# Which of the eight FFN down blocks is computed plainly: the first in place of the last, with the shared sums added slab by slab inside the last block

## The chip, the cores and the metric

One core of one Trainium2 chip runs the whole kernel. The metric is the device time of the kernel in microseconds (us). TensorE does the matrix products, VectorE and ScalarE the elementwise work, GpSimd part of the weight splitting, and SyncE's and ScalarE's queues issue the transfers.

## The reference, cut to what matters

Two transformer-like blocks run one after the other on 1024 tokens of width 1024. The change lies in the feed-forward part of the second one and in the gate behind it:

```
m = rmsnorm(h, g_mlp[i])
h = h + jnp.square(jax.nn.relu(m @ w_up[i])) @ w_down[i]     # D_FF = 4096
gate = jax.nn.sigmoid(rmsnorm(h, g_ple[i]) @ w_ple_gate[i])
h = h + gate * (p[i] @ w_ple_proj[i])
return rmsnorm(h, g_final)
```

## The kernel before, in words

**Numbers.** All products are made with split operands: a float32 value x is a high part (rounded to the format that TensorE multiplies) and a low part x minus high. A product is then three matmuls: high weight by high data, high weight by low data, low weight by high data. For weights ScalarE or GpSimd makes the high part, GpSimd the low part (`down_hi`, `down_part`, `plain_slab`), in a ring of eight entries (`w_hi`, `w_lo`) that TensorE frees as it goes. Weights come in slabs of 512 KB through SyncE's queue (`next_slab`) into a stage of two places; the transfer of a slab waits until the slab two before it is split.

**Up.** `f = relu(...)^2` is made in 16 pairs of feature tiles. Pairs 0 and 1 are plain, pairs 2 to 15 use a scheme with seven products in place of eight (`up_pair`; its products are numbered 1, 6, 5, 7, 2, 3, 4, the order `SEVEN`). Product 3 goes into the bank of product 5 and waits until VectorE has read that one (`c22`, L3367). Each finished pair is stored to DRAM (`f_kept`).

**Down.** The 4096 features are eight blocks of two pairs. In four slabs (s = 0 to 3) a block adds to `H`, each slab to two of its eight tiles. Blocks 0 to 6 use the seven-product scheme (`down`): 4 slabs of 7 products of 6 matmuls. For that VectorE and ScalarE must make, from the two stored pairs ("u"): four sums and differences (`diff`), seven high parts (`u_hi`), seven low parts (`u_lo`). And VectorE makes four sums of weights for each slab (`weight_sums`, behind the first addition of the slab before). VectorE adds each product into `H` or into `SHARED`, a sum that three of the four quarters of an output have in common (`down_added`). The work for block b+1 is spread over slabs 1 to 3 of block b (`next_u_steps`). A product can wait for VectorE: 2, 3 and 4 go into the banks of 1, 5 and 7 of the same slab:

```python
BANK = {1: 0, 2: 0, 6: 1, 5: 2, 3: 2, 7: 3, 4: 3}
BEFORE = {2: 1, 3: 5, 4: 7}
                    if j in BEFORE:
                        pe.wait_ge(s_dr, product_turn(b, s, BEFORE[j]))
```

Block 7 is plain (`last_down`): 4 slabs of 48 matmuls, with only four high and four low parts of u (1, 8, 2, 3) and no sums. While TensorE does it, VectorE adds `SHARED` into `H` (`shared_added`, 12 additions), adds the plain products, and finishes tile after tile of `H` for the gate (`last_tile`: `raw_lo`, L3276, and `raw_add`, L3285, with ScalarE's `raw_hi` and `raw_square` ahead of them). The projection (`PJ`, 4 MB) is loaded by ScalarE's queue at the end of block 6.

**Behind it.** The gate product (`product`, L991, on `XH2` and `XL2`) takes tile k of the data in order; `square_total` follows its first slab. The additions are counted by `s_dr`, the freed ring entries by `s_we`.

Every engine goes through its own instruction list in order, so an operation that waits holds all behind it on that engine.

Of the kernel before, what the change touches and what calls it, by code (L numbers as in the profile page):

```python
# [197 lines left out]
FFN_ORDER += [("down", _b, _s) for _b in range(DOWN_BLOCKS) for _s in range(4)]  # L198
FFN_ORDER += [("last", FFN_BLOCKS - 1, _s) for _s in range(4)]
# [27 lines left out]
for _n in range(pair_slab(PAIRS), N_PLE - 4):  # L227
    _uses(_n, 7, {6: _n + 1}, 1)
LAST_FREED = _freed
USED += USED[-1:] * (-len(USED) % RING)  # L230
for _n in range(N_PLE - 4, NSLAB):
    ENTRY[_n] = len(USED)
    USED += [("slab", _n + 1)] * 4
assert all(ENTRY[_n] % 4 == 0 for _n in range(N_PLE - 4, NSLAB))
DOWN_ADDS = 28 * DOWN_BLOCKS
# [61 lines left out]
def product_turn(b, s, j):  # L297
    return 7 * (4 * b + s) + SEVEN.index(j) + 1
# [23 lines left out]
def program(nc, x_t, pos, w, vec, rows, consts, p_t, out):  # L322
    ctx = ExitStack()
    with ctx:
# [146 lines left out]
        def head_square_at(k):  # L471
# [25 lines left out]
        u_even_at = {1: raw_at, 4: raw_at + 8 * kb, 5: xh_at + 48 * kb, 3: xh_at + 56 * kb, 6: xh_at, 2: xh_at + 8 * kb, 7: xh_at + 16 * kb}  # L497
        u_odd_at = {1: raw_at + 16 * kb, 6: raw_at + 24 * kb, 5: raw_at + 32 * kb, 7: raw_at + 40 * kb,
                    2: xh_at + 32 * kb, 3: xh_at + 40 * kb, 4: xh_at + 24 * kb}
        u_plain_at = {8: xh_at + 24 * kb, 1: xh_at + 32 * kb, 2: xh_at + 40 * kb, 3: xh_at + 48 * kb}  # L500
        u_at = {"even": u_even_at, "odd": u_odd_at, "plain": u_plain_at, "later": {5: raw_at + 48 * kb}}
        U_SPLIT = {(name, j): place(at_, f"ffn_u_{name}{j}", [P, 2, 2, HB], F32R)[0] for name, table in u_at.items() for j, at_ in table.items()}
        U_WHOLE = {(name, j): place(at_, f"ffn_whole_u_{name}{j}", [P, 2, 2, HB], F32)[0] for name, table in u_at.items() for j, at_ in table.items()}
        PJ = (place(xh_at, "ple_proj_a", [P, 6, TOK], F32)[0], place(xh_at + 56 * kb, "ple_proj_b", [P, 2, TOK], F32)[0])
# [21 lines left out]
        def u_name(b, j):  # L526
            if b == DOWN_BLOCKS:
                return "plain", j
            if b % 2:
                return "odd", j  # L530
            return "later" if j == 5 and b else "even", j
# [105 lines left out]
        s_hk = sem("h_kept_then_ffn_plain_u_loaded")  # L637
# [41 lines left out]
        s_u7 = Part(s_hk, 16 * KT)  # L679
# [59 lines left out]
        def _(sp):  # L739
# [57 lines left out]
            next_slab(d0)  # L797
            next_slab(d0 + 1)
# [6 lines left out]
            used(pair_use(p, 1))  # L805
            load(0, 3)
            used(pair_use(p, 2))
            load(0, 2)
            store(p, 0)
            store(p, 1)  # L810
            for b in range(DOWN_BLOCKS):
                if b == 0:
                    used(pair_use(p, 6))
                    stored(4)
                else:
                    sp.wait_ge(s_slab, FFN_AT["down", b - 1, 3] + 1)
                    stored(2 * b + 4)
# [4 lines left out]
            for n in range(d0 + 4 * DOWN_BLOCKS + 2, NSLAB):  # L822
                next_slab(n)
# [11 lines left out]
        def _(pool):  # L835
# [100 lines left out]
            def down_part(d, i):  # L936
                n, j = d0 + d, SEVEN[i]
# [10 lines left out]
            d0 = pair_slab(PAIRS)  # L948
            for c in range(2 * PLAIN_PAIRS):
                plain_slab(N_FFN + c, c)  # L950
            for p in range(PLAIN_PAIRS, PAIRS):
                for i in range(7):
                    pair_part(p, i)
            for d in range(4 * DOWN_BLOCKS):
                for i in range(7):
                    down_part(d, i)
            for turn, n in enumerate(range(N_PLE - 4, NSLAB)):
                plain_slab(n, 2 * PLAIN_PAIRS + turn)
# [11 lines left out]
        class Down:  # L970


            def wait(self, eng, k):
                eng.wait_ge(s_dr, DOWN_ADDS + k + 1)

        @block.tensor
        def _(pe):
# [724 lines left out]
            def down(b, s):  # L1702
                n = FFN_AT["down", b, s]
                e, d = ENTRY[n], 4 * b + s
                for i, j in enumerate(SEVEN):
# [19 lines left out]
            def last_down(q):  # L1725
                n = FFN_AT["last", FFN_BLOCKS - 1, q]
                e0 = ENTRY[n]
                pe.wait_ge(s_w_ready, 4 * (n + 1))
                if q == 0:
                    s_ul.wait(pe, len(LOWS))  # L1730
                    pe.wait_ge(s_dr, DOWN_ADDS - 7)
                elif q == 1:
                    pe.wait_ge(s_dr, DOWN_ADDS)
                for e in range(2):
                    if q >= 2:
                        pe.wait_ge(s_dr, DOWN_ADDS + 2 * (q - 2) + e + 1)
# [2031 lines left out]
```

## Time and profile before

| | |
|---|---|
| median of 3 runs | 2628.53 us (2624.53 to 2628.74) |
| profiled execution: time, span | 2624.4 us, 2622.5 us |
| granted TensorE clock, mean | 0.995 |
| busy: TensorE, VectorE, ScalarE, GpSimd | 97%, 66%, 44%, 43% |
| seven-product blocks of down begin at 2191.70 us, the plain one at 2472.09 us, the gate product at 2515.61 us | |

A duration is that of one instruction as the profile has it; instructions of one engine that follow each other without a gap overlap in the records by some 0.08 us on VectorE, so what counts on an engine that is never idle is the distance from start to start. "[2.31 <-DVE ffn_t L3367]" behind a row means that the engine sat idle for 2.31 us before it, until VectorE's instruction of line 3367 that writes ffn_t was done.

### The profile page before, as it was taken

The page shows a single profiled execution, that of the slowest core. Times are in us where ns is not written, and L with a number is a line of the kernel's source. Part 1 is how long each engine was busy: PE and PEld are TensorE (multiplying, and loading weights), DVE is VectorE, ACT ScalarE, POOL GpSimd, SP SyncE. Part 2 cuts the span into 40 slices and gives each one's busy share as a digit, 9 for nine tenths or more (in the row PEclk, how much of TensorE's full clock was granted, in tenths as well). Part 3 has the DMA queues.
Part 4 walks back from the last instruction along what each step waited for, and adds up shares of the span by engine and source line. Part 5 has one row for each costly group of instructions (what it writes and reads, how often), then busy time and mean ns, then how long its engine had stood idle before and what let it go on. Part 6 is the DMA issues. An engine that isn't in the chain of part 4 may idle for free.

```text
span 2622.5 us, 33254 instructions
## 1 busy us (share of the span) xinstructions
PE 2542.3 (97%) x12712; PEld 2022.7 (77%) x12712; DVE 1730.9 (66%) x2061; ACT 1147.0 (44%) x1757; POOL 1136.2 (43%) x1100
## 2 busy tenths in 40 slices
PE   8999999999999999999999999999999998999997
PEld 7877888687787787887676777767888887878886
DVE  7636763677748648658776455565556668999856
ACT  3527882336405305316275545463333334444232
POOL 4633344532342432432441222214645556777652
PEclk9999999999999999999999999999999999999999
DMA  3111002212212112111230001002133333322412
GB/s 140 49 44 33 25 25 86 92 47 101 65 49 81 57 48 73 64 49 61 84 129 25 33 25 33 25 25 97 49 126 107 113 113 121 121 98 104 161 41 81
DMA packets 58137, 189.93 MB, mean 72 GB/s; under 512 B 5952, under 2 KB 6336, under 8 KB 57984
## 3 DMA queue, kind: packets, MB, share of 16 engines
q1 hardware_dynamic: 44704, 143.67, 16.1%
q10 hardware_dynamic: 13280, 44.17, 4.7%
q8 instruction: 102, 1.67, 0.3%
q14 instruction: 51, 0.42, 0.1%
HBM read 158.33 MB, written 29.49 MB: 72 GB/s over the span
## 4 chain that ended last, share of the span: by engine, by line
PE 80%; DVE 11%; ACT 5%; issue 3%; POOL 1%; ACTq 0%; DMA 0%; DVEq 0%; POOLq 0%; SPq 0%
PE PS L991 38%; PE PS L1697 10%; PE PS L1720 8%; PE PS L1321 4%; PE PS L1228 3%; PE PS L1742 2%; PE PS L1554 1%; PE PS L1537 1%; PE PS L1354 1%; PE PS L1127 1%; PE PS L1364 1%; PE PS L1358 1%; PE PS L1141 1%; PE PS L1577 1%; PE PS L1670 1%
## 5 line engine op out<-in xcount | busy, mean ns | idle before, releaser
L839 POOL CAST w_hi<-w_stage 128x1024 fp32r<-128x1024 f32 x130 | 144.4, 1111 | 1046.9 <-PE PS L991 756.9
L842 POOL TENSOR_TENSOR w_lo<-w_stage,w_hi 128x256 fp32r<-128x256 f32 x520 | 494.0, 981 | 10.4
L991 PE MATMUL PS<-XH,w_hi 128*128 128x512 f32 x1216 | 386.6, 399 | 9.0 <-ACT ssd_z L2136 3.3
L991 PE MATMUL PS<-XL,w_hi 128*128 128x512 f32 x1216 | 375.5, 390 | 0.0
L991 PE MATMUL PS<-XH,w_lo 128*128 128x512 f32 x1216 | 375.0, 390 | 0.0
L991 PEld LDWEIGHTS PS<-XH,w_hi 128*128 128x128 f32 x1216 | 221.4, 188 | 65.5 <-issue 12.9
L991 PEld LDWEIGHTS PS<-XL,w_hi 128*128 128x128 f32 x1216 | 228.2, 188 | 48.8
L991 PEld LDWEIGHTS PS<-XH,w_lo 128*128 128x128 f32 x1216 | 228.2, 188 | 48.6
L946 POOL TENSOR_TENSOR w_lo<-w_sums,w_hi 128x256 fp32r<-128x256 f32 x112 | 126.1, 1138 | 59.7 <-ACT w_hi L2482 59.1
L1697 PE MATMUL PS<-ffn_token_sums,w_hi 128*128 128x512 f32 x448 | 138.0, 389 | 0.0
L1720 PE MATMUL PS<-ffn_u_even,w_hi 128*128 128x512 f32 x400 | 125.6, 395 | 5.3 <-DVE ffn_shared L3477 3.2
L934 POOL TENSOR_TENSOR w_lo<-up_w_sums,w_hi 128x512 fp32r<-128x512 f32 x56 | 82.7, 1478 | 80.7 <-ACT w_hi L2470 80.5
L2096 ACT ACTIVATE ssd_x<-ssd_conv 128x1024 f32<-128x1024 f32 x16 | 16.9, 1060 | 227.2 <-DVE ssd_conv L2924 222.5
L1697 PE MATMUL PS<-ffn_raw,w_hi 128*128 128x512 f32 x336 | 104.7, 393 | 2.3 <-DVE ffn_t L3367 2.3
L1720 PE MATMUL PS<-ffn_u_odd,w_hi 128*128 128x512 f32 x336 | 104.3, 392 | 1.1 <-DVE H L3479 0.4
L3479 DVE TENSOR_TENSOR H<-H,PS 128x512 f32<-128x512 f32 x140 | 93.4, 679 | 17.0 <-PE PS L1720 15.5
L1697 PEld LDWEIGHTS PS<-ffn_token_sums,w_hi 128*128 128x128 f32 x448 | 84.1, 188 | 17.4
L1720 PEld LDWEIGHTS PS<-ffn_u_even,w_hi 128*128 128x128 f32 x400 | 74.8, 190 | 25.4 <-issue 7.7
L2924 DVE SCALAR_TENSOR_TENSOR ssd_conv<-PS,VC,ssd_conv 128x1023 f32<-128x1023 f32 (+2 forms) x72 | 92.3, 1282 | 2.6
L2922 DVE TENSOR_SCALAR ssd_conv<-PS,VC 128x1024 f32<-128x1024 f32 x24 | 32.2, 1343 | 92.6 <-PE PS L991 92.5
L3240 DVE TENSOR_TENSOR sb_z<-sb_z,PS 128x1024 f32<-128x1024 f32 (+3 forms) x48 | 45.8, 954 | 67.3 <-PE PS L1554 67.0
L946 POOL TENSOR_TENSOR w_lo<-w_stage,w_hi 128x256 fp32r<-128x256 f32 x84 | 82.5, 990 | 15.3 <-ACT w_hi L2482 15.3
(492 smaller groups left out, 6105.1 us busy)
## 6 DMA issues: line engine op xcount, KB each, us to landing
w_stage<-w SPq DMA_DIRECT2D x202, 512.0 KB, 3.3
ssd_sum_rows<-sums_kept ACTq DMA_DIRECT2D x32, 512.0 KB, 3.8
f_kept<-ffn_t SPq DMA_DIRECT2D x32, 512.0 KB, 2.6
ffn_whole_u_even<-f_kept SPq DMA_DIRECT2D x16, 512.0 KB, 4.8
ffn_whole_u_odd<-f_kept SPq DMA_DIRECT2D x12, 512.0 KB, 5.4
H<-x_t ACTq DMA_DIRECT2D x8, 512.0 KB, 8.2
pj_kept<-ple_proj_tiles ACTq DMA_DIRECT2D x8, 512.0 KB, 2.6
h_kept<-H ACTq DMA_DIRECT2D x8, 512.0 KB, 3.6
```

Source lines behind the costliest of these rows:

```text
L839: nc.gpsimd.tensor_copy(w_hi[:, slot, :, :], w_stage[:, slot, :, :]).then_inc(s_w_hi, 1)
L842: nc.gpsimd.tensor_tensor(w_lo[:, slot, k:k + 2, :], w_stage[:, slot, k:k + 2, :], w_hi[:, slot, k:k + 2, :].bitcast(F32), ALU.subtract).t ...
L934: nc.gpsimd.tensor_tensor(ring(w_lo, e, 2), src, ring(w_hi, e, 2).bitcast(F32), ALU.subtract).then_inc(done, count)
L946: nc.gpsimd.tensor_tensor(ring(w_lo, e), src, ring(w_hi, e).bitcast(F32), ALU.subtract).then_inc(done, count)
L991: mm = nc.tensor.matmul(outs[:, half, :], wt[:, slot, k, :], a[:, k - first, half * HB:(half + 1) * HB], start=(k == whole[0] and wt is w_ ...
L1228: mm = nc.tensor.matmul(PS[:, 2 * (n % 2) + half, :], wt[:, n % 2, k, :], a[:, k, half_cols(half)], start=(k == 0 and wt is w_hi and a is ...
L1321: mm = nc.tensor.matmul(PS[:, half, :], wt[:, n % 2, k, :], a[:, k, half * HB:(half + 1) * HB], start=(k == 0 and wt is w_hi and a is XH), ...
L1697: mm = nc.tensor.matmul(PS[:, 4 * (p % 2) + BANK[j], :], ring(wt, e + 2 * i + k // 2, k % 2), up_acts(j, hl, k), start=(j not in BEFORE an ...
L1720: mm = nc.tensor.matmul(PS[:, 4 * (d % 2) + BANK[j], :], ring(wt, e + i, k), down_acts(b, j, k, hl), start=(j not in BEFORE and k == 0 and ...
L1742: mm = nc.tensor.matmul(PS[:, 4 * (q % 2) + 2 * e + half, :], ring(wt, e0 + k // 2, k % 2), down_acts(DOWN_BLOCKS, quad, t % 2, hl), start ...
L2924: ins = v.scalar_tensor_tensor(out=y[:, d:TOK], in0=src[:, 0:TOK - d], scalar=wcol(3 - d), in1=y[:, d:TOK], op0=ALU.mult, op1=ALU.add)
L3479: v.tensor_tensor(dst, dst, src, ALU.add).then_inc(s_dr, 1)
```

## The change

The order of the eight blocks is turned over at its ends. Block 0 is the plain one and comes first; blocks 1 to 7 use the seven-product scheme.

- At the end of the last up pair VectorE and ScalarE make only the four high and four low parts of block 0; the `diff`, `u_hi` and `u_lo` of block 1 are made while TensorE does the plain block, between the plain additions.
- Block 7 prepares no u. In its slabs VectorE does the three additions of `SHARED` for that slab behind product 6, the tile 2s-1 behind product 5, and the tile 2s behind product 4 (ScalarE's `gate_acts` are put between its `down_hi`).
- `PJ` is loaded by SyncE's queue: two tiles (1 MB) behind the loads of u at the start of block 1, six (3 MB) near the end of block 7. The places of u in memory are dealt out anew.

```diff
-FFN_ORDER += [("down", _b, _s) for _b in range(DOWN_BLOCKS) for _s in range(4)]
-FFN_ORDER += [("last", FFN_BLOCKS - 1, _s) for _s in range(4)]
+FFN_ORDER += [("plain", 0, _s) for _s in range(4)]
+FFN_ORDER += [("down", _b, _s) for _b in range(1, FFN_BLOCKS) for _s in range(4)]
...
                 for j in (1, 8, 3, 2):
                     load(b + 1, j)
-                for s in range(2, 6):
-                    next_slab(d0 + 4 * b + s)
+                if b == 1:
+                    sp.dma_start(PJ[0][:, :, :], pj_kept[0:2, :, :].rearrange("k p t -> p k t")).then_inc(s_pl, 16)
+                for c in range(2, 6):
+                    next_slab(n + c)
+            for n in range(PLAIN_DOWN + 4 * DOWN_BLOCKS + 2, N_PLE + 2):
+                next_slab(n)
+            used(USED[ENTRY[N_PLE - 1] + 2])
+            sp.dma_start(PJ[1][:, :, :], pj_kept[2:8, :, :].rearrange("k p t -> p k t")).then_inc(s_pl, 16)
...
-            def last_down(q):
+            def plain_down(q):
...
                     for t in range(4):
                         k = 4 * e + t
+                        if k % 2 == 0:
+                            pe.wait_ge(s_w_ready, 4 * n + k // 2 + 1)
+                        if q == 0 and e == 0 and t % 2 == 0:
+                            s_ul.wait(pe, t + 2)
...
+                    if not highs and d % 4 and i == 5:
+                        gate_acts(2 * (d % 4 - 1))
+                    if not highs and d % 4 > 1 and i == 1:
+                        gate_acts(2 * (d % 4 - 1) - 1)
...
+            def shared_added(s):
+                dve.wait_ge(s_dr, product_turn(FFN_BLOCKS - 1, s, 6))
+                for h in (H[:, 2 * s + 1, HB:TOK], H[:, 2 * s, HB:TOK], H[:, 2 * s + 1, 0:HB]):
+                    v.tensor_tensor(h, h, SHARED[:, s, :], ALU.add).then_inc(s_dv.sem, 1)
...
+                    if end and i == 1:
+                        shared_added(s)
+                    if end and s and i == 2:
+                        last_tile(2 * s - 1)
+                    if end and i == 6:
...
+                        last_tile(2 * s)
...
                 if last:
-                    diff(5, 0)
                     u_lo(1, 0)
-                    diff(6, 0)
+                    u_lo(8, 0)
...
+            diff(5, 1)
+            diff(6, 1)
+            plain_even(0)
+            diff(7, 1)
+            diff(4, 1)
+            u_lo(1, 1)
+            plain_odd(0)
```

## Rows read from the trace of the kernel before

**Rows 1.** The page, part 4: the chain that ended last, by engine

```profile
PE 80%; DVE 11%; ACT 5%; issue 3%; POOL 1%; ACTq 0%; DMA 0%; DVEq 0%; POOLq 0%; SPq 0%
```

**Rows 2.** Timeline of TensorE: start, duration, instruction, count, [idle before <- releaser]

```profile
2181.84 0.39 PE L1697 MATMUL PS<-ffn_raw,w_lo 128*128 128x512 f32 x1
2184.53 0.70 PE L1697 MATMUL PS<-ffn_raw,w_hi 128*128 128x512 f32 x2 [2.31 <-DVE ffn_t L3367]
...
2191.70 0.62 PE L1720 MATMUL PS<-ffn_u_even,w_hi 128*128 128x512 f32 x2
...
2202.35 1.19 PE L1720 MATMUL PS<-ffn_u_even,w_hi 128*128 128x512 f32 x2 [3.25 <-DVE ffn_shared L3477]
...
2237.79 0.61 PE L1720 MATMUL PS<-ffn_u_odd,w_hi 128*128 128x512 f32 x2
...
2434.01 0.62 PE L1720 MATMUL PS<-ffn_u_even,w_hi 128*128 128x512 f32 x2
...
2472.09 1.07 PE L1742 MATMUL PS<-ffn_u_plain,w_hi 128*128 128x512 f32 x4
...
2515.61 0.62 PE L991 MATMUL PS<-raw_hi,w_hi 128*128 128x512 f32 x2
```

**Rows 3.** Two stretches: length, busy time of each engine (instructions), granted clock, DMA share, GB/s

```profile
2192.00:2240.00 48.00, 43.20 (x178) 33.63 (x177) 45.51 (x63) 21.62 (x42) 34.57 (x32) 0.96 0.33 114
2240.00:2280.00 40.00, 39.44 (x172) 31.78 (x172) 37.17 (x57) 17.25 (x35) 30.00 (x29) 1.00 0.32 110
```

**Rows 4.** Timeline of VectorE in the last up pair

```profile
2177.30 1.23 DVE L3416 TENSOR_TENSOR ffn_whole_u_even<-ffn_whole_u_even,ffn_whole_u_even 128x1024 f32<-128x1024 f32 x1 [2.43 <-DMA ffn_whole_u_even<-f_kept]
2178.56 2.21 DVE L3422 TENSOR_TENSOR ffn_u_even<-ffn_whole_u_even,ffn_u_even 128x1024 fp32r<-128x1024 f32 x1
2180.69 2.31 DVE L3416 TENSOR_TENSOR ffn_whole_u_even<-ffn_whole_u_even,ffn_whole_u_even 128x1024 f32<-128x1024 f32 x1
...
2183.70 0.69 DVE L3367 TENSOR_TENSOR ffn_t<-ffn_t,PS 128x512 f32<-128x512 f32 x1
```

**Rows 5.** Timeline of VectorE in the down blocks and behind them

```profile
2436.43 0.68 DVE L3479 TENSOR_TENSOR ffn_shared<-ffn_shared,PS 128x512 f32<-128x512 f32 x1
2437.03 0.41 DVE L3448 TENSOR_TENSOR w_sums<-w_stage 128x256 f32<-128x256 f32 x1
...
2438.49 0.68 DVE L3479 TENSOR_TENSOR ffn_shared<-ffn_shared,PS 128x512 f32<-128x512 f32 x1
...
2445.70 0.66 DVE L3448 TENSOR_TENSOR w_sums<-w_stage 128x256 f32<-128x256 f32 x1
...
2472.30 0.69 DVE L3479 TENSOR_TENSOR H<-H,PS 128x512 f32<-128x512 f32 x1 [0.67 <-PE PS L1720]
2473.02 8.40 DVE L3489 TENSOR_TENSOR H<-H,ffn_shared 128x512 f32<-128x512 f32 x12
```

**Rows 6.** Three lines of VectorE: duration in ns, min/median/max

```profile
L3489 DVE TENSOR_TENSOR H<-H,ffn_shared x12: 676/678/1231, 2473.0 to 2480.7; 128x512 f32<-128x512 f32 x12
...
L3276 DVE SCALAR_TENSOR_TENSOR raw_lo<-H,VC,raw_hi x8: 1277/1478/1758, 2484.3 to 2519.7; 128x1024 fp32r<-128x1024 f32 x8
...
L3285 DVE TENSOR_TENSOR square_sum<-square_sum,ffn_t x12: 1218/1410/1761, 1832.7 to 2521.4; 128x1024 f32<-128x1024 f32 x12
```

**Rows 7.** SyncE's queue at block 6: issues, the two slabs' landing times; PJ

```profile
2434.21 2.51 SPq L782 DMA_DIRECT2D ffn_whole_u_plain<-f_kept  x4
2436.76 7.31 SPq L758 DMA_DIRECT2D w_stage<-w  x2
...
DMA to landing us min/median/max: 3.2/5.6/7.9
...
ple_proj_a<-pj_kept ACTq DMA_DIRECT2D x1, 3072.0 KB, 11.5
```

**Rows 8.** Timeline of TensorE: two gaps elsewhere, and the pace behind each

```profile
1769.99 0.73 PE L1554 MATMUL PS<-sb_softplus_hi,from_r 128*128 128x512 f32 x2 [1.65 <-DVE sb_softplus_lo L3258]
...
1778.67 0.94 PE L1554 MATMUL PS<-sb_softplus_hi,from_r 128*128 128x512 f32 x2 [2.24 <-DVE sb_softplus_lo L3258]
```

More of the change, by code:

```diff
@@ L526, in u_name, with u_loaded @@
         def u_name(b, j):
-            if b == DOWN_BLOCKS:
+            if b == 0:
                 return "plain", j
-            if b % 2:
-                return "odd", j
-            return "later" if j == 5 and b else "even", j
+            if b == 1 and j == 4:
+                return "first", j
+            return ("even", "odd")[b % 2], j
+        def u_loaded(b):
+            return 16 * (b // 2 + 1)
         def down_acts(b, j, i, hl):
@@ L805, in _ @@
             used(pair_use(p, 1))
+            load(0, 2)
             load(0, 3)
-            used(pair_use(p, 2))
-            load(0, 2)
             store(p, 0)
@@ L815, in _ @@
                 else:
[L816 to L817 removed]
+                    sp.wait_ge(s_slab, n)
+                    stored(PAIRS)
                 for j in (1, 8, 3, 2):
                     load(b + 1, j)
[L820 to L822 removed]
+                if b == 1:
[6 more added lines that the diff above has]
+            sp.dma_start(PJ[1][:, :, :], pj_kept[2:8, :, :].rearrange("k p t -> p k t")).then_inc(s_pl, 16)
+            for n in range(N_PLE + 2, NSLAB):
                 next_slab(n)
@@ L953, in _ @@
                     pair_part(p, i)
+            for c in range(4):
+                plain_slab(PLAIN_DOWN + c, 2 * PLAIN_PAIRS + c)
             for d in range(4 * DOWN_BLOCKS):
@@ L956, in _ @@
                     down_part(d, i)
-            for turn, n in enumerate(range(N_PLE - 4, NSLAB)):
-                plain_slab(n, 2 * PLAIN_PAIRS + turn)
+            for c, n in enumerate(range(N_PLE, NSLAB)):
+                plain_slab(n, 2 * PLAIN_PAIRS + 4 + c)
         class Tiles:
@@ L1750, in _ @@
                 up_pair(p)
-            for b in range(DOWN_BLOCKS):
+            for q in range(4):
+                plain_down(q)
+            for b in range(1, FFN_BLOCKS):
                 for s in range(4):
                     down(b, s)
-            for q in range(4):
-                last_down(q)
             for k in range(KT - 2):
@@ L2554, in _ @@
                 raw_square(ple, k)
+            for d in range(4 * DOWN_BLOCKS):
+                b = d // 4 + 1
+                highs = [j for j, b_ in HIGHS if b_ == b + 1]
+                for i in range(7):
+                    down_hi(d, i)
+                    if highs and d % 4 == 2 and i in (1, 3, 5):
+                        u_hi(highs[i // 2], b + 1)
+                    if highs and d % 4 == 3 and i in (1, 2, 4, 6):
+                        u_hi(highs[(1, 2, 4, 6).index(i) + 3], b + 1)
+                    if not highs and d % 4 and i == 5:
+                        gate_acts(2 * (d % 4 - 1))
+                    if not highs and d % 4 > 1 and i == 1:
+                        gate_acts(2 * (d % 4 - 1) - 1)
+            for k in range(5, KT):
+                gate_acts(k)
             raw_root(ple)
@@ L3475, in down_added @@
                         dve.wait_ge(s_dr, product_turn(b, s, 1 if j == 6 else 5))
-                    if j == 1 and b == 0:
+                    if end and j in (5, 3, 4):
+                        s_dv.wait(dve, 3 * s + {5: 1, 3: 2, 4: 3}[j])
+                    if j == 1 and b == 1:
                         v.tensor_copy(dst, src).then_inc(s_dr, 1)
```

210 lines of the change are left out of this document (81 added, 129 removed).

## Prediction

> **What bounds the kernel now.** I read the chain that ended last first: 80% of it is TensorE [rows 1], so the question is only where TensorE stands still, before and after. Then the timeline of TensorE at the block borders [rows 2]. From 2472.09 to 2515.61 the plain block runs 192 matmuls in 43.52 us, 0.2267 us each, without a pause; a product of six is 1.36 us, a slab of seven products 9.52, a block of four slabs 38.08. Against that pace the seven-product blocks show three things: block 0 takes 46.09 us (2191.70 to 2237.79), blocks 1 to 5 take 39.24 each (196.22 from 2237.79 to 2434.01), block 6 takes 38.08 (to 2472.09). VectorE is busy 37.17 of 40 us in blocks that prepare the next one [rows 3], so the 1.16 us that such a block loses is VectorE's; block 6 prepares only the light plain block and loses nothing. The gate product follows the plain block with no gap [rows 2].
>
> Ahead of block 0 TensorE loses more: the last matmul of product 2 of the last pair begins at 2181.84, and at full pace the 24 matmuls of products 3 and 4 would end at 2182.07 + 5.44 = 2187.51; they end at 2191.70. The wait of 2.31 us is for `c22`; VectorE came late to it because `diff`, `u_lo` and `diff` took from 2177.30 to 2183.0, the first behind a load, the other two at 2.2 and 2.3 us [rows 4]. In block 0 the longest wait, 3.25 us, is for the first addition, behind five low parts of u [rows 2], and the granted clock is 0.96 of full there [rows 3].
>
> **The change part by part.**
>
> *1. Entry into down: 11.0 us go.* Now only four high and low parts stand there. `u_lo` 1 can run from 2177 on, `u_lo` 8 about 1.2 us later; at 1.2 us each (they are 1024 wide like the 1.23 of [rows 4]) `c22` ends near 2181, before TensorE wants product 3 at 2182.07. If the second takes 2.2 us, TensorE waits up to 1 us. The last pair then saves 2191.70 - 2187.51 = 4.19. The plain block (43.52) needs nothing more of VectorE; there VectorE has 4 `diff`, 7 `u_lo` and 8 additions of 1.2 us and one `weight_sums`, 24 us, in 43.5, even if the loads of block 1's u come 8 us after the start. Block 1 then meets a VectorE that is free. In the sum: before, down was 46.09 + 5 x 39.24 + 38.08 + 43.52 = 323.9; after it is 43.52 + 6 x 39.24 + 38.08 + L = 317.0 + L, where six blocks (1 to 6) again prepare the next one and L is what block 7 loses. So 6.85 + 4.19 = 11.0 us are gained, bounds 10.0 and 11.0, less L.
>
> *2. Block 7: VectorE's work on the tiles now stands in front of TensorE: L = 10.8 us.* Before, `shared_added` and the tiles ran beside the plain block, which has no `BEFORE` waits within a slab. Now they stand between the addition of product 6 and those of 5 and 7, and TensorE's products 3 and 4 wait for exactly those two. Prices per instruction, start to start: an addition 0.60, four weight sums 1.46, an addition of `SHARED` 8.40 / 12 = 0.70 [rows 5]; `raw_lo` 1.30 and `raw_add` 1.22, the middle between shortest and median less the overlap of 0.08 [rows 6]. Block 6 shows VectorE taking up product 1 of a block 2.4 us after its start (2436.43 against 2434.01), because it still ends the block before [rows 2, 5]; so it will be at block 7. From the start of block 7 to the addition of product 7 in slab 3 VectorE has 25 additions (15.0), three `weight_sums` (4.4), twelve `SHARED` additions with four waits of 0.09 for product 6's sum (8.8), six `raw_lo` (7.8), five `raw_add` (6.1): 42.1. With 2.4 before, and 2.8 of waits for products (1.4 in slab 0, 0.7 in each of 1 and 2, mostly product 4, which cannot start before 7 is added), product 7 is added at 47.4. TensorE follows 0.14 later (`c22` ended at 2184.39, product 3 began at 2184.53 [rows 2, 4]) and needs 1.36: the block ends at 48.9 in place of 38.1. TensorE's gaps, walked slab by slab, are 1.3 us in slab 0 and pairs of 1.0 + 1.8, 2.3 + 1.8 and 0.9 + 1.8 in the others.
>
> Bounds: with the shortest durations everywhere (`SHARED` 0.60, `raw_lo` 1.20, `raw_add` 1.14) L is 8.6; with the medians of [rows 6] (1.40, 1.33) 11.9. What comes behind costs nothing: VectorE ends tile 7 at about 54, and TensorE wants it with the eighth step of the gate's first slab, at 48.9 + 9.5 = 58.4.
>
> *3. The clock.* A gap of 1.65 us was followed by two matmuls in 0.73 us, one of 2.24 by two in 0.94, and that of 3.25 by two in 1.19, against 0.62 at full pace [rows 2, 8]. The gap of 2.3 in slab 2 is at the edge. If the clock falls from 2.4 to 1.2 GHz for one product the loss hides in the wait that follows; if it falls at the 1.8 gaps too, product 4 takes twice 1.36 and the block 2.6 more. I take 0.5, bounds 0 and 2.6.
>
> *4. 1 MB of `PJ` in SyncE's queue: 2.0 us.* At block 6 the four loads of u go out from 2434.21, the first slab behind them at 2436.76, landing 7.9 us later, 10.7 after the block's start [rows 7]; VectorE wants it at 2445.70, 11.7 after [rows 5]. Only 1 us is to spare. 3 MB of `PJ` took 11.5 us [rows 7], so 1 MB takes up to 3.8; in front of the slab it brings it to 13.3 to 14.5. VectorE then stands at `weight_sums` for 2 to 3 us in slab 1 of block 1, with the additions for the product banks behind it, and in a block in which it has no slack. I take 2.0, since the transfers overlap in part; bounds 0 (the slab is not behind `PJ` after all) and 3.8. The other 3 MB go out some 9 us before the gate product and are used 11 us into it or later, and the slab behind them is wanted 21.8 us in: hidden, by about 8 us.
>
> *5. At nothing:* matmuls, transfers and splits are as many as before; `plain_down` now waits for its weights by quarters, which can only be earlier. ScalarE is at 17 of 40 us in blocks that prepare u [rows 3]; block 7 has none of those seven activations, and `gate_acts` puts up to four into a slab, ahead of high parts of weights that TensorE takes a slab later.
>
> Sum: -11.0 + 10.8 + 0.5 + 2.0 = +2.3 us on a profiled execution of 2624.4 us (span 2622.5). The median of the runs shown is 4.1 higher, so I put it on that: 2628.5 + 2.3 = 2630.8 us.
>
> **The rivals.**
>
> *Likeliest: an exchange of stalls.* The entry's stall goes, and block 7 gets one of the same size: 2631, in its own range 2626 to 2637 (all low: -11.0 + 8.6 = -2.4; all high: -10.0 + 11.9 + 2.6 + 3.8 = +8.3). Within 0.2% (5.3 us, about what a measurement of this kernel can tell from no change).
>
> *Faster.* The entry gains 11.0, and block 7 holds TensorE for less than 5 us. That needs the tile work to come later than I place it: if VectorE did it only beside the gate product, L would be the part of `SHARED` alone (1.3 in slab 0 and some 0.4 in two others, 2 in all), and the time 2628.5 - 11.0 + 2 = 2619.5, with the slab at `PJ` on time. For it: VectorE has 8 us to spare behind block 7. Against it: `last_tile` stands in front of the addition of 7 in the instruction order, and only its waits, not its place, can move. It decides at L + PJ below 5.7 us.
>
> *Slower by the clock.* In block 7 the pairs of gaps add up to 2.8, 4.1 and 2.7 us with one product between them. If that is enough for the lower level in slabs 1 to 3, and at the wait in block 1 as well, then -11.0 + 14.5 + 3.8 = +7.3: 2636. It decides when more than one slab of block 7 runs product 4 at 1.2 GHz.
>
> *Slower by contention.* `raw_lo` is 1.28 at its shortest and 1.76 at its longest, the addition of `SHARED` 0.68 and 1.23 [rows 6]; the long ones lie where GpSimd works. If all those in block 7 are long (`SHARED` 1.15, the others 1.68), L is 20.8 and the time 2628.5 - 11.0 + 20.8 + 2.0 = 2640. It would take GpSimd's work beside nearly each of them; GpSimd is busy 30 of 40 us in the down blocks [rows 3]. Against it: the medians are 1.48 and 0.68. The Trainium skill (GPSIMD Engine Reference, section 1, Specifications) says that GpSimd's SBUF interfaces are shared with VectorE and contended by instructions with two SBUF inputs. That speaks against this change, since the operations that it moves are of that kind and the additions that stay are not; the spread of the durations agrees with it.
>
> *The entry is not cured.* If `c22` is still late because the load of u lands later than 2177, 4 of the 11 us stay: 2635.
>
> **How the numbers follow.** Exchange 0.53. Faster 0.15. Clock 0.14, contention 0.10, entry not cured 0.08. Of the exchange a few per cent spill to the slow side, of the three slow ones about a quarter stays within 0.2%; faster 0.15, same 0.57, slower 0.28. The range 2622 to 2640 cuts off half of the faster case and the far end of contention.
>
> **What would show it.** The plain block begins near 2187.5 and lasts 43.5 us; no `c22` gap. Block 1 lasts some 41 us, with a wait for w_stage at VectorE's `weight_sums` in slab 1. Blocks 2 to 6 last 39.2. Block 7 lasts 47 to 50 us, with TensorE waiting for the additions of H. The gate product follows without a gap. Wrong would be: block 7 near 40 us (faster), or above 52 (slower), or a plain block that starts at 2191.

## The result, and the profile of the changed kernel

The changed kernel takes 2634.55 us (median of 7 runs, 2632.95 to 2637.3) against 2627.09 us (7 runs, 2624.53 to 2628.74) for the kernel before on the same chip: a ratio of 1.0029, 95% interval 1.0017 to 1.0041. It is slower, by 0.3%, 7.5 us. The forecast was +2.3 us, 2630.8 on a base of 2628.5, with a range of 2622 to 2640. The range holds the time, and the sign is the one forecast, but the likeliest outcome (0.57) was a change within 0.2%; slower than that had 0.28.

In the chain that ended last, TensorE has 75% and VectorE 14% [rows 1 had 80% and 11%]:

```profile
PE 75%; DVE 14%; ACT 5%; issue 4%; POOL 1%; DMA 0%; ACTq 0%; SPq 0%; DVEq 0%; POOLq 0%
```

The block borders, from the timeline of TensorE (start, duration, instruction, count, idle before it and its releaser); L1704 is the last up pair (products 2, 3 and 4 begin at 2181.99, 2184.71 and 2187.43), L1749 the plain block, L1727 the seven-product blocks, L998 the gate product:

```profile
2181.99 0.61 PE L1704 MATMUL PS<-ffn_raw,w_hi 128*128 128x512 f32 x2
...
2184.71 0.61 PE L1704 MATMUL PS<-ffn_raw,w_hi 128*128 128x512 f32 x2
...
2187.43 0.61 PE L1704 MATMUL PS<-ffn_token_sums,w_hi 128*128 128x512 f32 x2
...
2190.15 1.07 PE L1749 MATMUL PS<-ffn_u_plain,w_hi 128*128 128x512 f32 x4
...
2233.67 0.62 PE L1727 MATMUL PS<-ffn_u_odd,w_hi 128*128 128x512 f32 x2
...
2251.62 0.70 PE L1727 MATMUL PS<-ffn_u_odd,w_hi 128*128 128x512 f32 x2 [1.47 <-DVE H L3478]
...
2274.98 0.39 PE L1727 MATMUL PS<-ffn_u_even,w_hi 128*128 128x512 f32 x1
...
2471.03 0.62 PE L1727 MATMUL PS<-ffn_u_odd,w_hi 128*128 128x512 f32 x2
...
2480.51 1.05 PE L1727 MATMUL PS<-ffn_u_odd,w_hi 128*128 128x512 f32 x2 [2.52 <-DVE H L3478]
...
2496.46 0.70 PE L1727 MATMUL PS<-ffn_u_odd,w_hi 128*128 128x512 f32 x2 [1.86 <-DVE H L3478]
...
2498.04 1.05 PE L1727 MATMUL PS<-ffn_u_odd,w_hi 128*128 128x512 f32 x2
...
2510.76 0.70 PE L1727 MATMUL PS<-ffn_u_odd,w_hi 128*128 128x512 f32 x2 [1.84 <-DVE H L3478]
...
2525.33 0.70 PE L1727 MATMUL PS<-ffn_u_odd,w_hi 128*128 128x512 f32 x2 [2.07 <-DVE H L3478]
...
2526.80 0.63 PE L998 MATMUL PS<-raw_hi,w_hi 128*128 128x512 f32 x2
```

Read against [rows 2]: the last pair's product 3 starts at 2184.71 and product 4 ends 5.44 us later at 2190.15, the 24 matmuls at full pace and with no gap. Before, product 3 could have started at 2182.07, waited 2.31 us, and product 4 ended 9.63 us later, at 2191.70: 4.19 us are saved. The plain block takes 43.52. Block 1 takes 2274.98 - 2233.67 = 41.31. Blocks 2 to 6 take (2471.03 - 2274.98) / 5 = 39.21 each. Block 7 takes 2526.80 - 2471.03 = 55.77 where TensorE's work is 38.08: L is 17.7 us, forecast at 10.8. The gate product follows without a gap.

The spans of the two profiled runs differ by 10.7 us (2633.2 against 2622.5). The parts: entry -11.0, block 7 +17.7, block 1 +2.1, five blocks at 39.21 in place of 39.24 -0.2, behind the gate's start -0.5; the other 2.6 us are already there where product 3 of the last pair could start (2184.71 against 2182.07), ahead of all that was changed. Over all the profiled runs of this case the start of the plain block, where it comes first, scatters from 2188.5 to 2192.6 us, so that a single span is good to about 2 us only; borders within one trace are compared below.

Two stretches of VectorE in block 7, slab 0 and slab 3 (L3478 additions of products, L3457 additions of SHARED, L3277 `raw_lo`, L3286 `raw_add`):

```profile
2476.22 3.54 DVE L3457 TENSOR_TENSOR H<-H,ffn_shared 128x512 f32<-128x512 f32 x3
2479.69 2.06 DVE L3478 TENSOR_TENSOR H<-H,PS 128x512 f32<-128x512 f32 x3
...
2518.17 2.72 DVE L3457 TENSOR_TENSOR H<-H,ffn_shared 128x512 f32<-128x512 f32 x3
2520.81 0.68 DVE L3478 TENSOR_TENSOR H<-H,PS 128x512 f32<-128x512 f32 x1
2521.41 1.85 DVE L3277 SCALAR_TENSOR_TENSOR raw_lo<-H,VC,raw_hi 128x1024 fp32r<-128x1024 f32 x1
2523.17 1.41 DVE L3286 TENSOR_TENSOR square_sum<-square_sum,ffn_t 128x1024 f32<-128x1024 f32 x1
```

and GpSimd at slab 0:

```profile
2475.51 2.58 POOL L952 TENSOR_TENSOR w_lo<-w_sums,w_hi 128x256 fp32r<-128x256 f32 x3 [1.98 <-ACT w_hi L2488]
2478.05 1.17 POOL L952 TENSOR_TENSOR w_lo<-w_stage,w_hi 128x256 fp32r<-128x256 f32 x1
2479.18 1.17 POOL L952 TENSOR_TENSOR w_lo<-w_sums,w_hi 128x256 fp32r<-128x256 f32 x1
```

Three additions of SHARED take 3.54 us in slab 0, 1.18 each, while GpSimd makes low parts the whole time; the forecast had 2.1. The additions that read a product from PS (L3478) take no longer beside the same work: 0.67 to 0.69 each in the whole trace. In slab 1 the same three take 1.90, with GpSimd idle from 2490.4 to 2491.9. TensorE's first two matmuls behind the gap of 2.52 take 1.05 us against 0.62 at full pace.

### The profile page after: what moved, and what is told of

It is laid out like the page before. It is cut to its first block, busy times and chain, and to the rows that moved or that the text cites. A ratio compares the mean times of both kernels' runs of the same rounds, so it can differ in the third digit from the quotient of the medians.

```text
span 2633.2 us, 33267 instructions
## 1 busy us (share of the span) xinstructions
PE 2548.1 (97%) x12712; PEld 2026.9 (77%) x12712; DVE 1731.8 (66%) x2061; ACT 1147.1 (44%) x1757; POOL 1138.8 (43%) x1100
## 4 chain that ended last, share of the span: by engine, by line
PE 75%; DVE 14%; ACT 5%; issue 4%; POOL 1%; DMA 0%; ACTq 0%; SPq 0%; DVEq 0%; POOLq 0%
PE PS L998 38%; PE PS L1704 10%; PE PS L1328 4%; PE PS L1727 3%; PE PS L1235 3%; PE PS L1749 2%; DVE H L3478 2%; PE PS L1561 1%; PE PS L1134 1%; PE PS L1544 1%; PE PS L1361 1%; PE PS L1371 1%; PE PS L1365 1%; PE PS L1148 1%; PE PS L1584 1%
## 5 line engine op out<-in xcount | busy, mean ns | idle before, releaser
L998 PE MATMUL PS<-XH,w_hi 128*128 128x512 f32 x1216 | 387.6, 400 | 9.0 <-ACT ssd_z L2143 3.3
L998 PE MATMUL PS<-XL,w_hi 128*128 128x512 f32 x1216 | 376.2, 391 | 0.0
L998 PE MATMUL PS<-XH,w_lo 128*128 128x512 f32 x1216 | 375.6, 390 | 0.0
L998 PEld LDWEIGHTS PS<-XH,w_hi 128*128 128x128 f32 x1216 | 222.0, 188 | 65.5 <-issue 12.5
L998 PEld LDWEIGHTS PS<-XL,w_hi 128*128 128x128 f32 x1216 | 228.9, 188 | 48.9
L998 PEld LDWEIGHTS PS<-XH,w_lo 128*128 128x128 f32 x1216 | 228.6, 188 | 48.6
L1727 PE MATMUL PS<-ffn_u_odd,w_hi 128*128 128x512 f32 x432 | 138.0, 401 | 13.2 <-DVE H L3478 12.4
L1704 PE MATMUL PS<-ffn_token_sums,w_hi 128*128 128x512 f32 x448 | 137.9, 389 | 0.0
L1727 PEld LDWEIGHTS PS<-ffn_u_odd,w_hi 128*128 128x128 f32 x432 | 82.1, 193 | 36.3 <-POOL w_lo L952 10.3
L1727 PE MATMUL PS<-ffn_u_even,w_hi 128*128 128x512 f32 x336 | 104.3, 392 | 1.1 <-DVE H L3478 0.6
L3478 DVE TENSOR_TENSOR H<-H,PS 128x512 f32<-128x512 f32 x140 | 93.0, 678 | 18.4 <-PE PS L1727 17.1
L1704 PE MATMUL PS<-ffn_raw,w_hi 128*128 128x512 f32 x336 | 103.4, 389 | 0.0
L1704 PEld LDWEIGHTS PS<-ffn_token_sums,w_hi 128*128 128x128 f32 x448 | 84.1, 188 | 17.3
```

Source lines behind the costliest of these rows:

```text
L998: mm = nc.tensor.matmul(outs[:, half, :], wt[:, slot, k, :], a[:, k - first, half * HB:(half + 1) * HB], start=(k == whole[0] and wt is w_ ...
L1704: mm = nc.tensor.matmul(PS[:, 4 * (p % 2) + BANK[j], :], ring(wt, e + 2 * i + k // 2, k % 2), up_acts(j, hl, k), start=(j not in BEFORE an ...
L1727: mm = nc.tensor.matmul(PS[:, 4 * (d % 2) + BANK[j], :], ring(wt, e + i, k), down_acts(b, j, k, hl), start=(j not in BEFORE and k == 0 and ...
L3478: v.tensor_tensor(dst, dst, src, ALU.add).then_inc(s_dr, 1)
```

## The experiments

All times are compared with runs of the kernel before on the same chip: 2625.94 us (25 runs) for the first four kernels, 2626.36 us (28 runs) for the other four.

**Experiment 1: PJ behind the slabs.**

```diff
-                if b == 1:
-                    sp.dma_start(PJ[0][:, :, :], pj_kept[0:2, :, :].rearrange("k p t -> p k t")).then_inc(s_pl, 16)
                 for c in range(2, 6):
                     next_slab(n + c)
+                if b == 1:
+                    sp.dma_start(PJ[0][:, :, :], pj_kept[0:2, :, :].rearrange("k p t -> p k t")).then_inc(s_pl, 16)
```

> Only the 1 MB of PJ moves, behind the four slabs that SyncE's queue issues in block 1. If the 1.47 us gap of TensorE in slab 1 of block 1 comes from that transfer standing ahead of the slab, block 1 goes from 41.31 to 39.2 us and the time falls by 2.1 us (about 2632.5 against 2634.6). Rival: the gap comes from VectorE's own work in the first seven-product block (it enters with the plain block's last additions); then block 1 stays at 41.3 and the time at 2634.6. Block 7 stays at 55.8 in both.

Block 1 falls from 41.31 to 39.17 us (2232.00 to 2271.17), as blocks 2 to 6. Its gap in slab 1 is gone. The changed kernel and this one, VectorE in slab 1 of block 1:

```profile
2246.33 0.43 DVE L3440 TENSOR_TENSOR w_sums<-w_stage 128x256 f32<-128x256 f32 x1 [0.89 <-DMA w_stage<-w]
...
2247.13 0.96 DVE L3443 TENSOR_TENSOR w_sums<-w_stage 128x256 f32<-128x256 f32 x1
2248.01 0.96 DVE L3445 TENSOR_TENSOR w_sums<-w_stage,w_sums 128x256 f32<-128x256 f32 x1
```

```profile
2243.69 0.42 DVE L3440 TENSOR_TENSOR w_sums<-w_stage 128x256 f32<-128x256 f32 x1
...
2244.49 0.42 DVE L3443 TENSOR_TENSOR w_sums<-w_stage 128x256 f32<-128x256 f32 x1
2244.82 0.42 DVE L3445 TENSOR_TENSOR w_sums<-w_stage,w_sums 128x256 f32<-128x256 f32 x1
```

The wait for the slab is 0.89 us, and two of the sums that it pushed back take 0.96 in place of 0.42, another 1.1: GpSimd makes low parts beside them, from 2246.95 to 2248.69. The device time is 2633.51 us, ratio 1.0032 (1.0020 to 1.0043). The ratio does not show the 2.1 us; its interval is 6 us wide. The length of block 1 shows it, and all traces agree: 40.5 to 41.8 us where PJ stands ahead of the slabs (six traces), 39.14 to 39.17 where it does not (three). Block 7 takes 56.10 us here against 55.77, which is how much the same block differs between two traces.

**Experiment 2: the product additions first.** In block 7 the SHARED additions and the tile 2s-1 go behind the addition of product 7; their waits are changed to fit.

```diff
-                    if end and i == 1:
+                    if end and i == 3:
                         shared_added(s)
-                    if end and s and i == 2:
-                        last_tile(2 * s - 1)
+                        if s:
+                            last_tile(2 * s - 1)
...
```

> In block 7 the additions of product 5 and 7 come first on VectorE; the three SHARED additions and the tile 2s-1 come behind product 7. VectorE's work is the same, only its order differs. If L is set by the place of this work (it stands between product 6's addition and those that TensorE's products 3 and 4 wait for), the waits of VectorE for late products (0.8 to 2.7 us a slab) go and slab 3's share of SHARED and tile 5 falls behind product 7: by my walk with the durations of the trace after, block 7 falls from 55.8 to some 50 us, L from 17.7 to about 10 to 12 and the time by 6 to 7.5 us. Rival: L is only the sum of VectorE's work (clock and contention decide), then only the last slab's part, 2.7 + 3.6 us at most, is gained behind the block, and comes back as a wait of the gate product.

Block 7 falls from 55.77 to 51.71 us, L to 13.6; 2630.5 us, ratio 1.0018 (1.0009 to 1.0027). That is 4.1 of the expected 6 to 7.5 us. The rival allowed a gain in the last slab only, to come back as a wait of the gate product. Neither is so: slab 3 begins 37.3 us after the block in place of 41.9, it is itself no shorter (14.4 in place of 13.9), and the gate product runs without a gap. Place matters, but the stall has only moved: TensorE now waits at product 2 for the addition of product 1, which stands behind the tile of the slab before.

```profile
2486.33 0.70 PE L1727 MATMUL PS<-ffn_u_odd,w_hi 128*128 128x512 f32 x2 [1.09 <-DVE H L3478]
...
2498.94 0.77 PE L1727 MATMUL PS<-ffn_u_odd,w_hi 128*128 128x512 f32 x1 [4.20 <-DVE ffn_shared L3478]
...
2514.80 1.19 PE L1727 MATMUL PS<-ffn_u_odd,w_hi 128*128 128x512 f32 x2 [3.18 <-DVE ffn_shared L3478]
```

VectorE is busy 48.7 of the 51.7 us: in this order the block is nearly as long as VectorE's work. Of the 3.1 us in which it is idle, 1.8 are three waits for `raw_hi`, which ScalarE, idle until then, can begin only when VectorE has added product 3; the walk had left that out.

**Experiment 3: filling TensorE's gaps.** In block 7, ahead of the waits of products 3 and 4:

```diff
+                    if b == FFN_BLOCKS - 1 and i >= 5:
+                        for _ in range({5: 4, 6: 8}[i]):
+                            nc.tensor.matmul(PS[:, 4 * ((d + 1) % 2), :], ring(w_hi, e + i, 0), down_acts(b, j, 0, 0), start=True, stop=True)
```

> In block 7 TensorE makes 4 matmuls ahead of product 3's wait and 8 ahead of product 4's, into banks of the other parity that nothing reads, so that it stands still for under 1 us at a time. Additional work: 48 matmuls that belong to no result. Clock theory: the stretches at 0.43 us a matmul behind the gaps of 2.52, 1.86 and 1.84 us go, block 7 falls by some 2.9 us to 52.9, the granted clock there is 1.0. Rival (the slow products only fill a time in which VectorE would have been the bound anyway): block 7 falls by less than 1 us, although the clock is full; and if the fillers outlast a gap it grows by up to 0.5 us a slab.

The granted clock of block 7 rises from 0.91 to 1.00, no product runs at 0.43 us a matmul, and block 7 falls by 1.6 us, to 54.19 (2471.62 to 2525.81). The window of the changed kernel's block 7 and of this one's (length, busy time and instructions of TensorE, weight loads, VectorE, ScalarE, GpSimd, granted clock, DMA share, GB/s):

```profile
2471.03:2526.80 55.77, 44.80 (x170) 34.41 (x169) 49.88 (x68) 19.76 (x34) 35.32 (x36) 0.91 0.25 89
```

```profile
2471.62:2525.81 54.19, 50.56 (x218) 40.08 (x216) 49.31 (x68) 19.95 (x34) 35.14 (x36) 1.00 0.26 89
```

VectorE's busy time is 0.6 us shorter here, since other operations fell beside GpSimd's, so the clock's part is some 1.0 to 1.6 us: less than the 2.9 of one theory, and at or above the other's bound of 1. Two traces of the same block differ by 0.3 us (experiment 1). The device time does not resolve it (2634.5 us, ratio 1.0029, interval 1.0018 to 1.0040).

**Experiment 4: GpSimd made short.** In block 7, and for the weights of the gate, GpSimd handles 8 columns of 128:

```diff
...
+                c = 8 if d >= 4 * (DOWN_BLOCKS - 1) else 128
-                nc.gpsimd.tensor_tensor(ring(w_lo, e), src, ring(w_hi, e).bitcast(F32), ALU.subtract).then_inc(done, count)
+                nc.gpsimd.tensor_tensor(ring(w_lo, e)[:, :, 0:c], src[:, :, 0:c], ring(w_hi, e).bitcast(F32)[:, :, 0:c], ALU.subtract).then_inc(done, count)
```

> GpSimd's low parts for block 7's weights, and its high and low parts for the gate's slabs, are made of 8 columns in 128 (that part of the work is left out, the output is not the reference's); all instructions, waits and transfers stay. Contention theory: in block 7 the SHARED additions fall to 0.68 us each, raw_lo to 1.28 and raw_add to 1.2; by my account of the trace after, 4.3 us of block 7's 55.8 go, and a part of the 2.9 us of slow clock with them since the gaps get shorter: block 7 at 49 to 51.5. Rival: the durations stay long since ScalarE or the transfers cause them: block 7 stays at 55.8.

Block 7 falls from 55.77 to 46.63 us (2473.40 to 2520.03), by 9.1: more than either side of the expectation. 2624.56 us, ratio 0.9997 (0.9988 to 1.0006). L is 8.55. Groups of VectorE's instructions in block 7 of the changed kernel (count, busy us, mean ns, idle before):

```profile
L3478 DVE TENSOR_TENSOR H<-H,PS 128x512 f32<-128x512 f32 x22 | 14.3, 678 | 4.9 <-PE PS L1727 4.8
L3457 DVE TENSOR_TENSOR H<-H,ffn_shared 128x512 f32<-128x512 f32 x12 | 10.1, 891 | 0.1
L3277 DVE SCALAR_TENSOR_TENSOR raw_lo<-H,VC,raw_hi 128x1024 fp32r<-128x1024 f32 x6 | 8.2, 1374 | 0.0
L3286 DVE TENSOR_TENSOR square_sum<-square_sum,ffn_t 128x1024 f32<-128x1024 f32 x4 | 6.2, 1540 | 0.0
```

Block 7 of this kernel, the window and the groups:

```profile
2473.40:2520.03 46.63, 39.94 (x169) 31.00 (x168) 43.46 (x67) 19.96 (x34) 13.07 (x34) 1.00 0.25 79
```

```profile
L3481 DVE TENSOR_TENSOR H<-H,PS 128x512 f32<-128x512 f32 x21 | 13.7, 678 | 2.4 <-PE PS L1730 2.3
L3280 DVE SCALAR_TENSOR_TENSOR raw_lo<-H,VC,raw_hi 128x1024 fp32r<-128x1024 f32 x6 | 7.7, 1278 | 0.0
L3460 DVE TENSOR_TENSOR H<-H,ffn_shared 128x512 f32<-128x512 f32 x12 | 7.7, 691 | 0.1
...
L3289 DVE TENSOR_TENSOR square_sum<-square_sum,ffn_t 128x1024 f32<-128x1024 f32 x4 | 4.9, 1228 | 0.0
```

The additions from PS take 678 ns in both; the others fall to about their shortest values. VectorE is busy 43.46 us in place of 49.88, 6.4 less: 5.7 by shorter durations, 0.7 by one addition of block 6 fewer in the window. It waits 2.5 us less for products; together 8.9 of the 9.1. The granted clock is 1.00, and the longest gap 1.58 us: what experiment 3 gave back is within these 9.1, not beside them. The rival, that ScalarE or the transfers stretch VectorE, is excluded: ScalarE is busy 19.96 us against 19.76, and the DMA share is 0.25 in both.

**Experiment 5: a plain block at both ends.** From the changed kernel; block 7 becomes plain again with SHARED, tiles and PJ as in the kernel before, blocks 1 to 6 keep the seven-product scheme.

```diff
-PAIRS, PLAIN_PAIRS, DOWN_BLOCKS = 2 * FFN_BLOCKS, 2, FFN_BLOCKS - 1
+PAIRS, PLAIN_PAIRS, DOWN_BLOCKS, END = 2 * FFN_BLOCKS, 2, FFN_BLOCKS - 2, FFN_BLOCKS - 1
...
             for q in range(4):
-                plain_down(q)
-            for b in range(1, FFN_BLOCKS):
+                plain_down(0, q)
+            for b in range(1, END):
                 for s in range(4):
                     down(b, s)
+            for q in range(4):
+                plain_down(END, q)
```

> The plain block comes first, as in the changed kernel, and block 7 is plain as well, as in the kernel before: blocks 1 to 6 use the seven-product scheme, SHARED and the tiles are done beside the plain block 7, PJ is loaded by ScalarE's queue as before. One seven-product block less: 24 matmuls more in all. So the entry's gain stands alone, and its price is the second plain block. By the sum of the prediction without L: the last pair 4.19 us shorter, down 43.52 + 5 x 39.21 + 38.08 + 43.52 = 321.2 against 323.9: 6.9 us faster than the kernel before, about 2619. Rival (the entry's gain is an illusion of the trace and lies elsewhere, or the plain block at the end meets new waits): within 2 us of the kernel before.

2619.44 us (10 runs, 2617.14 to 2622.58), ratio 0.9978 (0.9968 to 0.9987): 6.9 us faster than the kernel before by the medians, 3.4 to 8.4 by the interval, which holds the 6.9 worked out, and faster than both kernels of this study. The borders:

```profile
2188.53 0.84 PE L1752 MATMUL PS<-ffn_u_plain,w_hi 128*128 128x512 f32 x3
...
2232.05 0.62 PE L1728 MATMUL PS<-ffn_u_odd,w_hi 128*128 128x512 f32 x2
...
2427.74 0.61 PE L1728 MATMUL PS<-ffn_u_even,w_hi 128*128 128x512 f32 x2
...
2465.82 0.84 PE L1752 MATMUL PS<-ffn_u_end,w_hi 128*128 128x512 f32 x3
...
2509.34 0.61 PE L999 MATMUL PS<-raw_hi,w_hi 128*128 128x512 f32 x2
```

43.52, five blocks of 39.14, 38.08, 43.52: 320.8 us where the kernel before has 323.9, with 5.4 us (24 matmuls of 0.2267) more of TensorE's work in it. With the last pair's 4.19 us that makes 7.3 in the trace.

**Experiment 6: the tiles behind block 7.** The SHARED additions stay. ScalarE's part of the tiles (`gate_acts`) moves behind the block as well.

```diff
-                    if end and s and i == 2:
-                        last_tile(2 * s - 1)
...
-                        last_tile(2 * s)
...
-            last_tile(KT - 1)
+            for k in range(KT):
+                last_tile(k)
```

> As the changed kernel, but all eight tiles (raw_hi, raw_square, raw_lo, raw_add) come behind block 7; the SHARED additions stay in it. It prices the two parts of L apart. Prediction's working: L of SHARED alone is 2 us with its shortest durations; with 1.15 us each where GpSimd works, about 4: block 7 at 40 to 42.5 us in place of 55.8, so the tiles are 13 us or more of the 17.7. The gate product then waits for its tiles: eight of them at about 2.6 us each against the 9.5 us of its first slab, 12 to 16 us more there, and the time is within 4 us of the changed kernel's. Rival (place of SHARED is the cause, the tiles lie in time that TensorE would lose anyway): block 7 stays above 50 us.

2634.15 us, ratio 1.0030 (1.0018 to 1.0042): the same time as the changed kernel. But block 7's products end at 2518.44, 47.0 us after 2471.44: L of SHARED alone is 8.9 us, not 2 and not 4; the rival's block above 50 us did not come either. The gate product then starts 2.5 us late, and its first slab takes 17.1 us (2520.97 to 2538.06) in place of 10.9 (2526.80 to 2537.70), where 12 to 16 us had been expected. It loses 8.7 us together, and 8.9 + 8.7 = 17.6 is what block 7 lost in the changed kernel. The twelve additions of SHARED in this kernel, by line; shortest, median and longest in ns:

```profile
L3453 DVE TENSOR_TENSOR H<-H,ffn_shared x12: 877/1220/1274, 2476.6 to 2513.6; 128x512 f32<-128x512 f32 x12
```

Nearly all of them now fall beside GpSimd's work, so 8.9 is the price of SHARED with stretched durations. The tiles cost about the same in both places: with this order, moving them only chose which wait shows them.

**Experiment 7: copies on GpSimd in place of subtractions.**

```diff
...
+                if d >= 4 * (DOWN_BLOCKS - 1):
+                    nc.gpsimd.tensor_copy(ring(w_lo, e), src).then_inc(done, count)
+                else:
...
```

> As the changed kernel, but for block 7's weights and the gate's first two slabs GpSimd makes its second part with a copy of the weights (one input) in place of the subtraction (two inputs), at full width; this part of the work is left out and the output is not the reference's. If what stretches VectorE's operations is GpSimd's reading of two inputs, they fall to 0.69 (SHARED) and 1.28 (raw_lo) as with the short operations, and block 7 to about 47 us. If any work of GpSimd at full width does it, they stay near 0.9 and 1.37 on average and block 7 falls only as far as the copies are shorter than the subtractions: 52 us or more.

Block 7 is 48.48 us (2472.29 to 2520.77), near the two-input side; 2626.36 us, ratio 1.0001 (0.9992 to 1.0010). At the place in slab 0 where three additions of SHARED took 3.54 us beside subtractions, they take 2.10 beside copies; VectorE's row and then GpSimd's rows of this kernel:

```profile
2477.03 2.10 DVE L3463 TENSOR_TENSOR H<-H,ffn_shared 128x512 f32<-128x512 f32 x3
```

```profile
2476.30 1.68 POOL L956 CAST w_lo<-w_sums 128x256 fp32r<-128x256 f32 x3 [2.30 <-ACT w_hi L2494]
2478.48 0.90 POOL L956 CAST w_lo<-w_stage 128x256 fp32r<-128x256 f32 x1 [0.50 <-ACT w_hi L2494]
```

But the mean of `raw_lo` stays at 1.35 us (SHARED 0.74), GpSimd, with copies, is busy 22.6 us in place of 35.3, and two of TensorE's waits (0.59 and 1.58 us) are for GpSimd's copies, not for VectorE. So the verdict is not clean: copies disturb less, and there is less of them. They are not without effect: where a copy meets VectorE's `raw_add` in slab 1, the two take 1.42 us in place of 1.22, and a copy beside `raw_lo`, 0.40 us alone, takes 1.50.

**Experiment 8: experiments 1 and 2 together.**

> The two repairs that showed in the first runs together: the additions of products 5 and 7 ahead of SHARED and tile 2s-1 in block 7 (block 7 at 51.7), and the 1 MB of PJ behind the slabs of block 1 (block 1 at 39.2). If they add: 4.1 + 2.1 us less than the changed kernel, about 2628.5, still 2 to 3 us above the kernel before, because L is about 13.6 and the entry gives back 11.0. If they don't add: 2630.5, as with the first alone.

Block 1 takes 39.16, block 7 51.83: in the trace the two repairs add. The time is 2630.16 us, ratio 1.0015 (1.0006 to 1.0024) where experiment 2 alone had 1.0018. That is 1.7 us above the expected 2628.5, within an interval 4.7 us wide: the device times neither confirm nor exclude that the second repair adds. The two repairs are not enough: L stays at 13.8, above the 11.0 that the entry gives.

## Why the forecast held and where it failed

The forecast came within its range, but not by its sum: the term that decides was 6.9 us too small, and the time came in only because the range was wide. By the prediction's own signs, block 7 above 52 us is the slower case.

**The entry (term 1): right.** No gap for `c22`, the last pair at full pace, the plain block at 43.52, block 1 without a wait in slab 0. The last pair is 4.19 us shorter, and block 0's 6.85 us are gone; the 2.1 us that block 1 loses have another cause (term 4). Experiment 5 shows the entry without the exit: 6.9 us were worked out for it, and 6.9 came by the medians (3.4 to 8.4 by the interval). One sign was badly chosen: a plain block that starts at 2191 was to speak against the entry. It starts between 2188.5 and 2192.6 in the traces that have it first, with no gap ahead of it; only the distance from product 3 of the last pair tells.

**Block 7 (term 2): the right mechanism, mis-sized.** The forecast said that VectorE's work on SHARED and the tiles would stand in front of the additions that products 3 and 4 wait for. Each of TensorE's seven gaps in block 7 waits for an addition of H. Forecast 10.8, bounds 8.6 to 11.9, measured 17.7. With GpSimd's operations short, L is 8.55: the lower bound, made with the shortest durations, is right to 0.1 us. So what failed is VectorE's time per instruction, together with the waits and the slow clock that follow from it (9.1 us in all, of which 5.7 are VectorE's own stretch). The step that failed is the price list: "an addition of `SHARED` 8.40 / 12 = 0.70". That row [rows 5] lies from 2473.0 to 2481.4 in the kernel before, where GpSimd, by its timeline in the kernel before, was done at 2475.45 and then idle for 7.82 us:

```profile
2473.07 2.38 POOL L920 TENSOR_TENSOR w_lo<-w_stage,w_hi 128x256 fp32r<-128x256 f32 x2
2483.27 0.74 POOL L909 CAST w_hi<-w_stage 128x256 fp32r<-128x256 f32 x2 [7.82 <-PE PS L1742]
```

So only the additions of the first 2.4 us, three or four of the twelve, could meet GpSimd's work there, and the longest took 1.23 us [rows 6]. The change moved the additions to just behind product 6, which is where ScalarE has made the high parts and GpSimd makes the low ones. In the changed kernel they take 0.89 on average (long in slabs 0 and 3, at their shortest in the other two, where they meet a pause of GpSimd), in experiment 6, where nearly all are beside GpSimd, 1.22 by the median.

**The contention rival (0.10, 2640): its mechanism is the cause of the miss, its extent about three quarters of what it assumed.** It assumed that nearly each operation is long, L = 20.8; 17.7 came, from a base of 8.6: (17.7 - 8.6) / (20.8 - 8.6) is 75%, the clock's share included. The argument against it, that the medians are 1.48 and 0.68, carries no weight, since medians are those of the place where the operations stood before. The rule given there from the Trainium skill (GPSIMD Engine Reference, section 1, Specifications), that instructions with two SBUF inputs contend for the shared interfaces, agrees with experiment 4: additions with one SBUF input keep their 678 ns, those with two take 891 on average with GpSimd at full width and 691 without.

**The clock (term 3): forecast 0.5, bounds 0 to 2.6; some 1.0 to 1.6 by experiment 3.** Within its bounds, above the value taken. It is contained in the 17.7 of block 7 and is not added to it. Three stretches run at 1.2 GHz: one at the gap of 2.52 us in slab 0, which the forecast had at 1.3 us, one behind slab 1's pair of 1.07 and 1.86, one inside product 4 of slab 2 behind 0.78 and 1.84. Slab 3's pair of 0.83 and 2.07, and with GpSimd short a pair of 1.58 and 1.32, were followed by full pace; in experiment 1 slab 3's pair was 1.50 and 2.09 and 1.2 GHz followed at once. The clock rival had product 4 of slabs 1 to 3 at the lower level and 2.6 us more; three stretches came, but mostly at other products and for less. The prediction judged a gap by the two matmuls just behind it. That misses a loss that comes later, and its own rows had one: behind the gap of 2.31 us in the kernel before, the first two matmuls take 0.70, but from 2185.4 to 2188.7 TensorE runs at 1.2 GHz, and 1.7 of the last pair's 4.19 us are lost there.

```profile
2185.37 1.05 PE L1697 MATMUL PS<-ffn_raw,w_hi 128*128 128x512 f32 x2
```

**PJ in the queue (term 4): right.** 2.0 forecast, 2.1 by experiment 1. Only 0.9 of it is the wait for the slab; 1.1 is that the sums pushed back fell beside GpSimd's work, which the forecast did not have.

**What comes behind: right.** The gate product follows without a gap, and the stretch behind its start is 0.5 us shorter.

By the measured terms the sum is -11.0 + 17.7 + 2.1 - 0.5 = +8.3, against +7.5 by the medians. "Faster" at L + PJ below 5.7 us was not within reach with this order of the additions: in experiment 6 SHARED alone costs more than that.

## What to carry to other kernels

A duration is a property of a place, not only of an instruction: before pricing work that moves, look at what the neighbour engines do at the place it comes from and at the place it goes to. If the two differ, let the longest duration seen set the bound, and do not rest on the median. And a block with cheaper TensorE work is only cheaper where VectorE has room. Here a plain block at both ends, with 24 matmuls more, beats the kernel before by 6.9 us and the changed one by about twice that, because at both ends of the stage VectorE has other work to do.

## What the runs showed of the hardware that was not expected

- VectorE's operations with two SBUF inputs and GpSimd's work stretch each other. Beside GpSimd's subtractions of 128x256 an addition of 128x512 goes from 0.68 to 1.22 us (longest 1.27), `raw_lo` from 1.28 to 1.85, `raw_add` from 1.22 to 1.77, a sum of weights of 128x256 from 0.42 to 0.96. An addition with one input in PS stays between 0.67 and 0.69 in every trace here. GpSimd's subtraction of 128x256, 0.74 us alone, takes 1.17 in the rows above.
- The full step of VectorE, 0.54 us, is the same for operations whose lengths differ by three times. It goes with the length of GpSimd's instruction instead: 0.2 beside a copy of 0.40 us (experiment 7), 0.54 beside a subtraction of 0.74, and 1.14 beside one of 128x512 in the up stage, 1.29 us long. In each case that is GpSimd's instruction less 0.15 to 0.2 us. No run varied this by itself. VectorE and GpSimd in the kernel before; the first takes 0.69 alone:

```profile
2166.67 1.83 DVE L3386 SCALAR_TENSOR_TENSOR ffn_t<-ffn_t,root 128x512 f32<-128x512 f32 x1
```

```profile
2166.66 1.29 POOL L934 TENSOR_TENSOR w_lo<-up_w_sums,w_hi 128x512 fp32r<-128x512 f32 x1 [0.98 <-ACT w_hi L2470]
```

- Not every meeting costs VectorE. In slab 1 of the changed kernel's block 7 `raw_lo` keeps its 1.28 us while GpSimd works throughout, and GpSimd's subtractions take 1.35 each:

```profile
2492.76 1.28 DVE L3277 SCALAR_TENSOR_TENSOR raw_lo<-H,VC,raw_hi 128x1024 fp32r<-128x1024 f32 x1
```

```profile
2491.93 2.70 POOL L952 TENSOR_TENSOR w_lo<-w_sums,w_hi 128x256 fp32r<-128x256 f32 x2 [1.55 <-ACT w_hi L2488]
```

- A gap of TensorE of 1.86 us behind one of 1.07 is followed by full pace for 1.2 us and then by a stretch at 1.2 GHz, so the loss does not stand beside the gap. It is read in the rows further on, 1.05 us for two matmuls in place of 0.62.
